# Ten adaLN chunks multiplied and added up on VectorE beside the keys' and values' projections, and another order of the layers' pieces

## The reference, cut to what matters

```python
sh1, sc1, gt1, sh2, sc2, gt2 = jnp.split((jax.nn.silu(c) @ w_ada + b_ada)[:, None, :], ADA_CHUNKS, axis=-1)
csh1, csc1, cgt1, csh2, csc2, cgt2 = jnp.split(jax.nn.silu(c_ctx) @ w_ada + b_ada, ADA_CHUNKS, axis=-1)
rq, rk, rv, rg, mq, mk, mv, mo, mg, gr, gm = _split_in(_modulate(x, norm1_g, sh1, sc1) @ w_in)
crq, crk, crv, crg, cmq, cmk, cmv, cmo, cmg, cgr, cgm = _split_in(_modulate(ctx, norm1_g, csh1, csc1) @ w_in)
...
x = x + gt1 * _merge(_retention_out(yr, rg), _mlstm_out(ym, mo), gr, gm, w_ret_out, w_mlstm_out, w_out)
x = x + gt2 * _peer(_modulate(x, norm2_g, sh2, sc2), peer_query, peer_keys, peer_down, peer_up)
```

## Time and profile before

| | us |
|---|---|
| median of three runs | 4055.27 (4050.76 to 4063.96) |
| the profiled execution | 4056.81 |
| its span, first to last instruction | 4055.2 |

### The profile page before, as it was taken

One profiled execution on the slowest core, in us unless ns is written; L12 is line 12 of the kernel. 1 busy time (PEld: TensorE's weight loads), 2 busy tenths in 40 slices (PEclk: granted clock), 3 DMA queues, 4 the chain that ended last, 5 costly groups with the idle time before them and its releaser, 6 DMA issues.

```text
span 4055.2 us, 50512 instructions
## 1 busy us (share of the span) xinstructions
PE 3824.5 (94%) x21362; PEld 3212.6 (79%) x21362; DVE 2238.6 (55%) x2974; ACT 1571.7 (39%) x1558; POOL 101.1 (2%) x145
## 2 busy tenths in 40 slices
PE   7998989899889977999999989999999999999998
PEld 6676766777667655888888879999999999998886
DVE  3346533334554344226574557967745555657777
ACT  3344434334343343113554343335543333333333
POOL 0000000000000000001000000000000000000000
PEclk9999999999999988999999999999999999999999
DMA  6545566654555651224345644556666666666664
GB/s 252 212 157 198 186 238 236 222 210 152 211 194 207 257 186 47 100 89 160 131 144 212 253 153 176 187 190 221 234 229 223 222 223 222 219 228 247 240 237 176
DMA packets 117960, 799.34 MB, mean 197 GB/s; under 512 B 13136, under 2 KB 13520, under 8 KB 29456
## 3 DMA queue, kind: packets, MB, share of 16 engines
q1 hardware_dynamic: 96704, 692.73, 47.5%
q0 software_dynamic: 18768, 82.96, 5.5%
q10 hardware_dynamic: 2304, 20.97, 1.3%
HBM read 752.57 MB, written 44.04 MB: 196 GB/s over the span
## 4 chain that ended last, share of the span: by engine, by line
PE 55%; DVE 5%; ACT 1%; DMA 1%; issue 1%; DVEq 0%; POOLq 0%; ACTq 0%; POOL 0%; SPq 0%
PE ps L270 17%; PE ps L272 17%; PE ps L271 17%; DVE ring_r L284 1%; PE ps L1602 1%; DMA ring<-in_stream_dram 1%; PE ps L1462 1%; DVE z L2993 0%; DVE act L2757 0%; PE ps L1411 0%; PE ps L1425 0%; DVE z L2989 0%; DVEq L251 0%; DVE z L3047 0%; DVE z L3044 0%
## 5 line engine op out<-in xcount | busy, mean ns | idle before, releaser
L284 DVE TENSOR_TENSOR ring_r<-ring,high 128x2048 fp32r<-128x2048 f32 x384 | 878.8, 2291 | 718.8 <-ACT high L278 715.0
L278 ACT CAST high<-ring 128x2048 fp32r<-128x2048 f32 x384 | 733.9, 1912 | 1263.8 <-DMA ring<-in_stream_dram 1254.9
L2227 DVE TENSOR_TENSOR ring_r<-ring,high 128x2048 fp32r<-128x2048 f32 x176 | 403.1, 2291 | 700.7 <-ACT high L1710 699.3
L270 PE MATMUL ps<-high,z_r 128*128 128x512 f32 x1856 | 734.9, 396 | 15.5 <-DVE ring_r L2227 13.3
L272 PE MATMUL ps<-high,act_r 128*128 128x512 f32 x1888 | 743.0, 394 | 0.0
L271 PE MATMUL ps<-ring_r,z_r 128*128 128x512 f32 x1856 | 728.7, 393 | 0.0
L271 PE MATMUL ps<-act_r,high 128*128 128x256 f32 x2496 | 706.7, 283 | 0.0
L270 PE MATMUL ps<-act_r,high 128*128 128x256 f32 x2304 | 656.5, 285 | 9.7 <-DVE ring_r L284 9.3
L272 PE MATMUL ps<-act_r,ring_r 128*128 128x256 f32 x2304 | 652.5, 283 | 0.0
L270 PE MATMUL ps<-high,h_r 128*128 128x512 f32 x1472 | 600.6, 408 | 52.0 <-DVE ring_r L2227 21.1
L1710 ACT CAST high<-ring 128x2048 fp32r<-128x2048 f32 x176 | 335.3, 1908 | 683.5 <-DMA ring<-in_stream_dram 683.1
(11 more groups left out here) (465 smaller groups left out, 3116.9 us busy)
## 6 DMA issues: line engine op xcount, KB each, us to landing
ring<-in_stream_dram SPq DMA_DIRECT2D x656, 1024.0 KB, 4.8
hidden<-z POOLq DMA_DIRECT2D x32, 512.0 KB, 4.2
gate_matrix<-z ACTq DMA_DIRECT2D x8, 2048.0 KB, 7.2
r<-gate_matrix POOLq DMA_DIRECT2D x32, 512.0 KB, 6.6
z<-hidden POOLq DMA_DIRECT2D x32, 512.0 KB, 7.0
r<-in_w_ple_dram POOLq DMA_DIRECT2D x2, 2048.0 KB, 12.5
merge_gates<-r ACTq DMA_DIRECT2D x8, 512.0 KB, 4.8
r<-merge_gates POOLq DMA_DIRECT2D x4, 1024.0 KB, 5.8
```

What stands on the lines that cost most here:

```text
L270: pe.matmul(out, lhs[0], rhs[0], start=start, stop=False)
L278: sc.copy(high[:, j, :], ring[:, j, :]).then_inc(piece_high[j], 1)
L284: dve.tensor_tensor(ring_r[:, j, :], ring[:, j, :], high[:, j, :], ALU.subtract).then_inc(piece_low[j], 1)
L2227: dve.tensor_tensor(ring_r[:, b, :], ring[:, b, :], high[:, b, :], ALU.subtract).then_inc(piece_low[b], 1)
```

## The change

- The layers keep 14 adaLN chunks, 7 each, at the slots of `ADA_SLOTS`, where a chunk's four slots need not follow each other.
- The other ten are loaded in `kv` and in `mvmk`'s first chunk, two per weight chunk (`load_ada`), into the ring's buffers between weight pieces: every buffer takes weights, adaLN, adaLN, weights. VectorE multiplies an adaLN piece with silu(c) per partition and adds it up (`ada_part`, 4 instructions on 128x512, each dependent on the one before; sums for c alone). TensorE adds the partitions with a column of ones (`sum_ada`), eight sums after the second piece of `mvmk`'s first chunk and two in `mqrq`.
- Input chunks 0 and 1 of a layer are interleaved (`IN_PIECES`), output pieces stand in another order, and two pairs of them are multiplied by halves (`parts_of`); TensorE's waits for tiles are set to it.
- VectorE's selection rounds stand in slots 32 to 37 (`ROUNDS`), and two of its rotations earlier. `H1_AT` moves by one slot.
- `mvmk` and `mqrq` begin without a barrier (`FLOWING`).

```diff
-OUT_PIECES = [(0, 0), (1, 0), (0, 3), (1, 3), (0, 1), (0, 2), (1, 1), (1, 2)] + [(c, j) for c in (2, 3) for j in range(PIECES)]
-LAYER_PIECES = [("in", c, j) for c in ORD for j in range(PIECES)] + [("out", c, j) for c, j in OUT_PIECES] + \
+IN_PIECES = [(0, 0), (0, 1), (0, 2), (1, 0), (1, 1), (1, 2), (0, 3), (1, 3)] + [(i, j) for i in range(2, N_IN) for j in range(PIECES)]
...
+OUT_PIECES = [(0, 0), (1, 0), (0, 3), (1, 3), (0, 1), (1, 1), (0, 2), (1, 2)] + [(c, j) for c in (2, 3) for j in range(PIECES)]
...
-ADA_SLOT = (1, 6, 11, 16, 28, 33, 38, 43, 58, 63, 68, 73)
+ADA_SLOTS = ((5, 8, 9, 11), (14, 15, 16, 17), (28, 30, 31, 32), (35, 36, 37, 38), (41, 43, 44, 45), (57, 59, 61, 63), (76, 78, 80, 83))
...
+        KV_ADA = 5
...
+        def kv_chunk(m):
+
+            return (0, 2 * PAIR0["kv"] + m, ADA_L + 2 * min(m, KV_ADA))
...
-        H1_AT = (63, 65, 69, 73)
+        H1_AT = (64, 66, 69, 73)
+        ROUNDS = (32, 32, 33, 34, 35, 35, 36, 37)
...
+        FLOWING = ("mvmk", "mqrq", "scan")
...
+            for m in range(KV_ADA):
+                load_ada(m, 0, 0)
+                load_weights(m, 3)
+                load_ada(m, 1, 0)
+                load_ada(m, 0, 1)
+                load_weights(m + 1, 0)
+                load_ada(m, 1, 1)
+                load_ada(m, 0, 2)
+                load_weights(m + 1, 1)
+                load_ada(m, 1, 2)
+                load_ada(m, 0, 3)
+                load_weights(m + 1, 2)
+                load_ada(m, 1, 3)
...
+                        if q == OUT_SLOT + 4:
+                            return [(q, (0, 1)), (q + 1, (0, 1))]
+                        if q == OUT_SLOT + 5:
+                            return [(q - 1, (2, 3)), (q, (2, 3))]
...
+                                pe.wait_ge(tile_low, TILES(l, "mixed", (3, 3, 9, 6)[j]))
...
+                        elif c == 0:
+                            pe.wait_ge(tile_low, TILES(l, "mixed", 7))
...
-                                if q < 4 and (j == 0 or l):
-                                    pe.wait_ge(tile_low, TILES(l, "x", (8 if l == 0 else 2 * (j + 1))))
...
+                        for n in range(n_):
+                            for b in range(4):
+                                mm = pe.matmul(ps[:, bank, 4 * n + b:4 * n + b + 1], ada_sums(first + n)[:, b * P:(b + 1) * P], ones[:, 0:1], start=True, stop=True)
+                        mm.then_inc(ada_turned, 1)
...
                         if name == "mvmk" and par == 1:
                             pe.wait_ge(evac[0], EVAC0[name] + 4)
+                            pe.wait_ge(ada_done, ADA_L + 1)
...
+                                elif name == "mvmk" and par == 0 and j == 1:
+                                    pe.wait_ge(evac[1], EVAC0[name])
+                                    pe.wait_ge(piece_used[3], ada_used(3, 1))
+                                    sum_ada(0, 8, 7)
...
-                    stream_split(sc, split_act, "mvmk", 1, out_m, looped=False)
+                    for m in (4, 5):
+                        split_act(sc, kv_chunk(m), (3,))
+                        split_act(sc, kv_chunk(m + 1), range(3))
+                        sc.wait_ge(piece_used[3], place(kv_chunk(m), 1, 1))
+                        out_m(0, m % 2)
...
+                    def ada_part(m, i, j):
...
+                        for q in range(PIECE_KT):
+                            k = PIECE_KT * j + q
+                            w, c = ring[:, j, q * CHUNK:(q + 1) * CHUNK], col(C_SILU + 2 * k)
+                            if k == 0:
+                                a = dve.tensor_scalar(o, w, c, None, ALU.mult)
+                            else:
+                                a = dve.scalar_tensor_tensor(o, w, c, o, ALU.mult, ALU.add)
+                            if q < PIECE_KT - 1:
+                                chain(dve, "dve", a)
+                        a.then_inc(piece_used[j], 1)
...
+                    def stream_kv(m, evacuate):
...
+                        ada_part(m, 0, 0)
+                        low(m, 3)
+                        ada_part(m, 1, 0)
+                        ada_part(m, 0, 1)
+                        low(m + 1, 0)
+                        ada_part(m, 1, 1)
+                        ada_part(m, 0, 2)
+                        low(m + 1, 1)
+                        dve.wait_ge(piece_used[3], place(kv_chunk(m), 1, 1))
+                        evacuate()
+                        ada_part(m, 1, 2)
+                        ada_part(m, 0, 3)
+                        low(m + 1, 2)
+                        ada_part(m, 1, 3)
```

More of the change, by code:

```diff
@@ L913, in _, with load_weights, load_ada @@
             gates1 = 2 * PAIR0["merge"] + ADA_CHUNKS
-            with sp.Fori(2 * PAIR0["kv"] + ADA_CHUNKS, gates1) as c:
+            def load_weights(m, j):
+                sp.wait_ge(piece_used[j], sum(kv_chunk(m)))
+                sp.dma_start(ring[:, j, :], t["stream"][2 * PAIR0["kv"] + ADA_CHUNKS + m, j]).then_inc(piece_full[j], 16)
+            def load_ada(m, i, j):
+                sp.wait_ge(piece_used[j], ada_used(m, i) - 1)
+                sp.dma_start(ring[:, j, :], t["stream"][ada_place(ADA_L + 2 * m + i), j]).then_inc(piece_full[j], 16)
+            for j in range(3):
+                load_weights(0, j)
+            for m in range(KV_ADA):
[11 more added lines that the diff above has]
+                load_ada(m, 1, 3)
+            load_weights(KV_ADA, 3)
+            with sp.Fori(2 * PAIR0["kv"] + ADA_CHUNKS + KV_ADA + 1, gates1) as c:
                 load_chunk(c, c)
@@ L1320, in _ @@
+                        for q in range(SLOTS):
+                            for p, blocks in parts_of(q):
+                                products(l, p, blocks)
                             if l:
@@ L1362, in _ @@
                             pe.wait_ge(evac[0], EVAC0[name] + 4)
+                            pe.wait_ge(ada_done, ADA_L + 1)
+                        if name == "mqrq" and par == 0:
+                            pe.wait_ge(evac[1], EVAC0[name])
                         if name == "mqrq" and par == 1:
@@ L1702, in _ @@
             for n, (name, l) in enumerate(STAGES):
-                begin(sc, n, () if name == "scan" else ALL)
+                begin(sc, n, () if name in FLOWING else ALL)
                 f0 = full[n]
@@ L2208, in _ @@
                 if after:
-                    split_act(sc, (0, 2 * PAIR0[after], ADA_BEFORE[after]), range(3))
+                    split_act(sc, kv_chunk(0), range(3))
                 end(sc, "act")
@@ L2690, in out_kv @@
                                .then_inc(evac[par], 1)
-                    stream_split(dve, split_dve, "kv", 2, out_kv, looped=False)
+                    for m in range(4):
+                        stream_kv(m, lambda: out_kv(m // 2, m % 2))
                 elif name == "mvmk":
@@ L3181, in _ @@
                 if after:
-                    split_dve(dve, (0, 2 * PAIR0[after], ADA_BEFORE[after]), range(3))
+                    split_dve(dve, kv_chunk(0), range(3))
                 end(dve, "dve")
```

192 lines of the change are left out of this document (116 added, 76 removed).

## The result

The changed kernel takes 3956.9 us (median of four runs, 3952.8 to 3964.6) against 4053.3 us: a ratio of 0.9759, with a 95% interval from 0.9736 to 0.9783. The forecast was 3959. Most terms of the sum were close.

A forecast was written before the change was run, and what follows sets the result against it. TensorE, busy 94% of the span, was taken to bound the kernel. Layers -141 us and the stages after them +43.5 made -97.5: 4056.8 to 3959 us, range 3922 to 4022.

The forecast's parts named there:

- Step 1: Layers: ten adaLN chunks leave TensorE, 40 pieces and ten turns of bare time, -50 us.
- step 4: Layers: with fewer waits, half of the 36 us lost to TensorE's lower clock goes, -19 us.
- Step 2: Layers: long waits for x tiles, mixed tiles (piece 60) and piece 72's low part are covered, -36.5 us.
- Step 3: Layers: short waits, arising where adaLN stands at a slot and the one before, mostly go, -35.5 us.
- Rival A: Layers: the short waits move elsewhere instead of going, 4006 us in all; chance 0.18.
- Step 5: kv: added adaLN loads and 160 dependent VectorE instructions make the serial buffer chain outlast TensorE's chunk, +7 us.
- Step 6: First mvmk chunk: TensorE waits 5.3 us for the last sum, then adds up 32 columns; with lateness, +14 us.
- Step 7: Before mvmk's second chunk: TensorE stands still 16.7 us for copies out of PSUM behind ScalarE's cast, +15 us.
- Rival B: kv doesn't starve, so the cost behind the layers is 25 us instead of 43.5, 3940 in all; chance 0.14.
- D: kv: VectorE's 160 instructions run several times longer beside other traffic, making it slower, 4287 us; chance 0.04.
- E: Layers: the ring stays as short as before, only -50 stands against +43.5, 4050 us, no change; chance 0.04.
- C: Layers: the clock pays nothing, 3978 us in all; chance 0.06.

The follow-up runs named there:

- e2: The kernel before with ten of its adaLN chunks left out, the other fourteen in the old order of pieces; 3954.3 us, ratio 0.9756.
- e11: e7 without the halves, the second pieces of output chunks 0 and 1 multiplied whole; 3936.4 us, ratio 0.971.
- e8: The changed kernel with its fourteen adaLN chunks at the slots of e2; 3981.0 us, ratio 0.9818.
- e7: The changed kernel with the layers' adaLN pieces from slot 28 on at every second slot; 3922.8 us, ratio 0.9679.
- e3: The changed kernel with one VectorE instruction per adaLN piece in kv and mvmk instead of four, all loads kept; 3936.8 us, ratio 0.9701.
- e6: The changed kernel with each VectorE low part in kv and mvmk one step later, behind the next two adaLN pieces; 3939.3 us, ratio 0.9721.
- e4: The changed kernel with ScalarE's two copies of mvmk's first chunk ahead of its cast of piece (5, 2); 3941.6 us, ratio 0.9724.
- e1: The changed kernel without the ten adaLN chunks of kv and mvmk, neither loaded, multiplied nor added up; 3908.1 us, ratio 0.9639.
- e5: The changed kernel with TensorE's eight sums behind the third piece of mvmk's first chunk instead of the second; 3946.3 us, ratio 0.9736.
- e10: e9 with the eight sums in two blocks of four, behind mvmk's first chunk's second and third pieces; 3893.1 us, ratio 0.9606.
- e12: e10 with a layer's first two adaLN chunks and its last at other slots, the first at 3, 5, 7, 9; 3898.5 us, ratio 0.9622.
- e9: The changed kernel with e7's slots, e4's copies and e6's low parts together; 3896.0 us, ratio 0.9607.

## Why the prediction was right, point by point

| term | predicted | measured |
|---|---|---|
| 1: ten chunks off TensorE | -50 | about -55.7 (400 instructions fewer) |
| 2 and 3: waits in the layers | -72 | -70.1 (107.1 to 37.0 idle) |
| 4: clock in the layers | -19 | about -27.8 |
| 1 to 4, the layers | -141 | -153.6 |
| 5: `kv` | +7 | +6.4 |
| 6: first `mvmk` chunk, 7: standstill, clock, last sums | +36.5 | +38.6 |
| rest | 0 | +8.6 |

- **Step 1** and step 4 together are the busy time, which fell by 83.5 us. The trace parts them: with each moment of TensorE's busy time weighted by the clock granted then, 42.1 us of it were lost to the lower level before and 14.3 after. That is 27.8 for the clock, and 55.7 are left for step 1 (a weighting, so good to some us). A part of what 50 left out shows in the rows. The first matmul behind an adaLN piece is followed after 0.34 us (44.21 in the earlier trace rows to the first row below), and not after the usual 0.23 (the two rows below), some 4.5 us in 40 pieces:

```profile
44.55 0.39 PE L271 MATMUL ps<-ring_r,h_r 128*128 128x512 f32 x1
44.78 0.40 PE L272 MATMUL ps<-high,act_r 128*128 128x512 f32 x1
```
- **Step 2**'s size held and its cause only in part. Piece 60's wait was put down to the halves and to the loads; e2 took 13.9 of the 17.3 us away without halves, with slots 58 to 61 empty, and e11 gives the halves 6.9 where adaLN stands at every second slot. The x tiles' 8.2 us do belong to the order of pieces (e2 keeps them, e8 doesn't have them). Piece 72's 11.0 us belong to the slots, as forecast: they are gone in the changed kernel and back in e8, with adaLN at 68 to 71 (5.3 and 4.0).
- **Step 3**'s rule was shown right by e7 and e8 for the attention's slots, but for slot 33 (above), which it counted among them. Its prices were off within and close in sum (-33.6 with step 2 as forecast, for -35.5). Slot 37, priced at 2.2 us a layer, has no wait; slot 38 waits 4.1 instead of 3.2; the 3.3 us of slot 35 became 4.7 in slot 36. The small waits for low parts are 7.5 us, where 6.4 were to be left. Rival A, that waits move instead of going, was right for some 2 us a layer, at slots 36 and 38.
- **Step 4** is the term that was mis-sized: about 28, not 19. The loss was 42 us and not 36, and I let half of it go with two thirds of the waits; two thirds of it went too (42.1 to 14.3, where the waits went from 107.1 to 37.0). The Trainium skill ("TensorE: Matmul & The Clock Gate", section "What's actually happening") puts the ramp's penalty under 1% of a typical kernel span and advises against fitting a particular count of slow matmuls. By the same weighting the kernel before loses 51.9 of its 4055.2 us, 1.3%, and to leave the term out would have missed more than a quarter of the gain.
- **Step 5** was right in mechanism (e3, e6) and in size. The instructions took 0.77 us each in the chain, not 0.72 (the 8 of one row above took 6.13), and a load 4.8 us from issue to landing (the median of 32 in `kv`), as priced with 4.75. What I called "strictly serial" was an order, though: e6 breaks the series for nothing.
- **Step 6**: the wait is 5.25 us (5.3), the sums 13.65 us (7.7). What failed is the price of 32 x 0.24 at full clock. The 5.5 us put down for the clock stood for low stretches behind the waits. Measured, 6.0 us more than the price were spent in the sums, 2.3 in the piece behind them (13.3 us for 11.0) and 1.4 in the chunk behind the standstill (47.75 us for 46.31).
- **Step 7**: 14.4 us (16.7, though the terms written there add up to 16.5), so +13.0 instead of +15. e4 shows the order on ScalarE to be the cause.
- **The rest** was 8.6 us longer, which no term held. The same code behind `mqrq` took 2179.3 us in e1, 2178.3 in e3, 2173.4 in e4 and between 2173 and 2177 in the rest of the runs looked at, against 2173.5 before. The changed kernel's 2182.1 is the longest of them all. Since the code is the same it is put down to the spread of runs, which is argued and not shown. It hid that the layers gained 12.6 us more than forecast: without it the profiled span would be 3946.6 us, and the forecast would be 11 us off instead of 2. That it came within 2 us is luck.

Rival B's condition, that `kv` doesn't starve, is met by e6; rivals D and E fell with 0.77 us an instruction and 37 us of waits, and C with the 28 us of step 4.

## What to carry to other kernels

Take the waits one by one and ask what is queued on both sides: the greatest single gain after the change's own was in moving light work two slots apart, not in making less of it. Where work is moved beside a stream that shares its buffers, write down the chain through one buffer and through the engine that frees it; an engine busy for 60% of a stage can still be what the stage waits for, and a reorder of its list may remove that at no cost (17.9 us here). And look at each copy out of PSUM that the next matmul needs: nothing that waits for a load belongs in front of it.

## What the runs showed of the hardware that was not expected

- One-column fp32 matmuls behind one another let TensorE's clock fall to its lower level, 1.2 GHz, with no idle time before or among them: 32 of them took 11.4 us in e5. Two blocks of 16 took 3.5 us each in e10, 0.22 us a matmul, and the clock fell behind one of the two.
- The ring's loads of 1 MB took 4.8 us each beside one another in `kv`, and 9.0 us (12.6 at most) in e12 while GpSimd's loads kept the DMA engines busy with them.
- How long the lower level lasts after the same wait varies from run to run. In the first 23.6 us of the layers, behind the start's wait of 8 us, the changed kernel and e9 have the same code and did 129 and 86 matmuls:

```profile
23.40:47.00 23.60, 23.59 (x129) 20.43 (x129) 9.41 (x9) 10.64 (x19) 1.63 (x2) 0.94 0.58 231
```

```profile
23.40:47.00 23.60, 23.59 (x86) 20.12 (x87) 7.11 (x8) 9.61 (x19) 1.63 (x2) 0.60 0.48 187
```

The clock of that stretch was 0.94 in one and 0.60 in the other: it rose at 26.4 us in the changed kernel and at 42.4 us in e9, with TensorE busy all the while. This may be a part of why the medians of one kernel spread, and it is why idle time and busy time are told apart here.
